# A decoder and PEER kernel on one core: the last attention's copies and splits in another order, the last four choices handed on one at a time, loops in TensorE's expert stage, and the final norm's weights spread on chip

## The chip, the core and the metric

The kernel runs on one core of a Trainium2 chip. The metric is device time in microseconds (us) of one execution, first to last instruction with what lies around them; the time before is the median of three runs. The core has five engines that run on their own and meet through semaphores: TensorE (PE in the profile; PEld is its weight load), VectorE (DVE), ScalarE (ACT), GpSimd (POOL) and SyncE (SP). Transfers run on 16 DMA engines.

## The reference, cut to what matters

The program is a two-layer block (pooling mixer, differential attention, four gated feed-forwards), followed by a second block: a hybrid attention mixer and a PEER layer that fetches expert rows by index. The change touches the mixer and the PEER layer of the second block and the last norm.

```python
def second_block(x, c, w_ada, b_ada, norm_attn, norm_ffn, w_in, w_out, rel_bias,
              peer_wq, peer_subkeys, peer_u, peer_v, norm_final):
    ...
        x = x + g1[:, None, :] * hybrid_mixer(h, w_in[l], w_out[l], rel_bias)
        h = modulate(rms_norm(x, norm_ffn[l]), sh2, sc2)
        x = x + g2[:, None, :] * peer_ffn(h, peer_wq[l], peer_subkeys[l], peer_u[l], peer_v[l])
    return rms_norm(x, norm_final)

def peer_ffn(h, w_query, sub_keys, u_emb, v_emb):
        ...
        e_idx = jnp.take_along_axis(cand_idx, pos, axis=-1)      # 128 experts for each of 256 tokens
        g = jax.nn.softmax(g_s, axis=-1)
        u = u_emb[e_idx]
        act = jax.nn.gelu(jnp.einsum('btd,bthkd->bthk', hc, u).astype(jnp.float32), approximate=False)
        return jnp.einsum('bthk,bthkd->btd', (g * act).astype(h.dtype), v_emb[e_idx])
```

All is float32, 256 tokens of width 1024. Every token picks 8 heads x 16 experts; each expert has a row of `u` and a row of `v`.

## The kernel before, in words

**Large products.** A weight chunk lands in `WR`; ACT writes its high part to `WH` (L1365) and DVE the rest to `WL` (L1877), half a chunk at a time. This is a *split*, in two pieces of 128x1024. PE then does three products per weight tile. `WH` and `WL` have two halves, so the split of half j + 2 waits until PE has used half j, and PE waits for the split. DVE copies a finished half out of PSUM (L1947, `post_copy`); PE may use that bank again, and the queries and keys in it, only then.

**The last attention** (L1160 to L1250 on PE, L1696 to L1746 on ACT, L2413 to L2474 on DVE) has 8 steps, each a pair of heads, pipelined by hand. In step i, PE does scores of pair i + 1 (L1167), the weighted sum of pair i - 1 (L1190, L1192) and the transposes of pair i (L1180, L1181). ACT does the exponentials (L1701), the normalising (L1710), the copy of the transposes (L1717, `pair_pt`) and of the result (L1721). DVE does bias and maxima (L2437, L2441) and the low part of the result (L2451), and beside these eight rounds of a selection of 64 keys, `topk` (L2419, L2422), three rounds per step. Between these each engine carries its share of halves 5 to 13 of the input product (steps 0 to 4), and in steps 5 to 7 of the output product. On each engine the order is that of the code: nothing is scheduled by a tool, every engine goes through its list and stops at each wait.

In step 0 DVE did three rounds of `topk`, then the copy of half 5 and the split of half 7, the copy of half 6 and the split of half 8. In steps 5 to 7 ACT did its part of a split ahead of `pair_pt`.

**The expert stage.** 64 groups (`GROUPS` is 32 for each of the two token tiles), each of 4 choices. POOL issues one indirect DMA per choice (L668): 128 rows of 8 KB, an expert's `u` beside its `v`. Four buffers of 4 choices each form a ring (`early_uv`, `late_uv`), and a gather waits until PE has used that buffer, four groups earlier (`v_used`). For a group DVE makes four dot products (L2525), each when its rows have landed; ACT takes one Gelu of the four (L1806); DVE multiplies by the gates (L2532); ACT writes four scaled identities `diag` (L1811); PE does eight products into PSUM (L1321, each in two passes, so 16 instructions). PE's code has groups 0 to 39 written out, then a loop of five rounds over groups 40 to 59, then groups 60 to 63 written out. DVE and ACT loop over groups 44 to 63.

**The end.** When tile 0's 32 groups are done, DVE adds them to `xt` and later scales by the final norm (`finish`); SP stores both halves of tile 0 as soon as they are ready. The norm's weights `gfin` come by one DMA that writes all 128 partitions (512 KB), issued when all choices are made. After group 63, `add_experts(1)` waits for all of PE's products, adds (L2577, L2578), ACT sums squares (L1844), DVE scales (L2585) and SP stores the second tile (L530).

## Time and profile before

| what | us |
|---|---|
| median of 3 runs (lowest to highest) | 1969.83 (1968.81 to 1976.73) |
| the profiled execution, device time | 1972.46 |
| its span, first to last instruction | 1971.2 |
| PE busy, share of the span | 1769.3, 90% |
| DVE busy, share of the span | 1280.4, 65% |
| ACT busy, share of the span | 799.0, 41% |

A share of busy time is a mean over stages with different limits. The chain that ended last is 57% PE and 25% DMA over the whole span; it is DMA in the last third, where the experts are fetched. What a step is worth is read from the stage it stands in: who waits there, for whom, and who waits for him.

### The profile page before, as it was taken

What the parts mean: (1) busy time and instruction counts of PE and PEld (TensorE: products, weight loads), DVE (VectorE), ACT (ScalarE), POOL (GpSimd) and SP (SyncE); (2) the same over time, 40 slices, a digit from 0 to 9 for tenths busy, and PEclk for the clock granted to TensorE, in tenths of its full rate; (3) what the DMA queues carried; (4) which work ended last, traced back from release to release, by engine and by line L of the source; (5) the groups of instructions that cost most, each with busy time, mean ns of one, the idle gap of its engine ahead of it and who ended that gap; (6) DMA issues with size and microseconds to landing.
All of it is one profiled execution on the core that took longest, in us unless ns stands there. A gap on an engine that the chain in (4) does not pass through costs nothing.

```text
span 1971.2 us, 23001 instructions
## 1 busy us (share of the span) xinstructions
PE 1769.3 (90%) x8104; PEld 1301.5 (66%) x8104; DVE 1280.4 (65%) x2235; ACT 799.0 (41%) x1442; POOL 651.3 (33%) x602
## 2 busy tenths in 40 slices
PE   7999999999999999999999889699888787878786
PEld 5887898888888888988887888575433333333232
DVE  4566866556465656676654676678688788855554
ACT  5444435544354436565443456442322232311111
POOL 4442551044214451144440012023443343333330
PEclk9999999999999999999999899899998888889999
DMA  8999985799999999769996965299999999999995
GB/s 261 319 363 392 316 289 219 262 337 366 334 321 334 373 348 343 265 224 312 353 355 220 280 209 163 87 385 351 394 419 420 419 420 420 419 421 421 420 421 215
DMA packets 247211, 650.00 MB, mean 330 GB/s; under 512 B 14881, under 2 KB 156498, under 8 KB 214354
## 3 DMA queue, kind: packets, MB, share of 16 engines
q1 hardware_dynamic: 200146, 346.15, 51.5%
q0 software_dynamic: 46304, 301.52, 38.3%
q10 hardware_dynamic: 672, 1.18, 0.3%
q8 instruction: 52, 0.85, 0.2%
q14 instruction: 37, 0.30, 0.0%
HBM read 643.56 MB, written 139.48 MB: 397 GB/s over the span
## 4 chain that ended last, share of the span: by engine, by line
PE 57%; DMA 25%; DVE 10%; ACT 4%; issue 3%; SPq 1%; POOL 0%; ACTq 0%; DVEq 0%
DMA late_uv<-uv_rows,M 11%; PE P L1321 9%; DMA early_uv<-uv_rows,M 7%; PE PX L828 6%; PE PX L830 6%; PE PX L829 6%; PE P L734 4%; PE P L736 4%; PE P L735 4%; DMA WR<-in_ffn_w_up 4%; DVE WL L1877 2%; PE P L683 2%; PE P L684 2%; PE P L685 2%; DMA WR<-in_ffn_w_down 2%
## 5 line engine op out<-in xcount | busy, mean ns | idle before, releaser
L1877 DVE TENSOR_TENSOR WL<-WR,WH 128x1024 fp32r<-128x1024 f32 (+1 forms) x246 | 325.2, 1363 | 205.4 <-ACT WH L1365 205.3
L1365 ACT ACTIVATE WH<-WR 128x1024 fp32r<-128x1024 f32 (+1 forms) x272 | 270.8, 1044 | 345.1 <-PE P L736 116.3
L1321 PE MATMUL P<-early_uv,M 128*128 128x512 f32 x576 | 284.7, 652 | 72.0 <-ACT M L1811 72.0
L828 PE MATMUL PX<-WH,hTh 128*128 128x512 f32 x704 | 280.7, 399 | 7.6 <-DVE WL L1885 5.1
L830 PE MATMUL PX<-WH,hTl 128*128 128x512 f32 x704 | 275.7, 392 | 0.0
L829 PE MATMUL PX<-WL,hTh 128*128 128x512 f32 x704 | 275.1, 391 | 0.0
L1321 PEld LDWEIGHTS P<-early_uv,M 128*128 128x128 f32 x576 | 117.3, 209 | 233.8 <-issue 143.1
L1321 PE MATMUL P<-late_uv,M 128*128 128x512 f32 x448 | 220.7, 651 | 55.3 <-ACT M L1811 55.0
L1892 DVE TENSOR_TENSOR WL<-WR,WH 128x1024 fp32r<-128x1024 f32 x128 | 177.8, 1430 | 138.4 <-ACT WH L1374 138.4
L668 POOL DMA_INDIRECT early_uv<-uv_rows,M x144 | 138.7, 963 | 297.1 <-PE P L1321 189.5
L2525 DVE CUSTOM_DVE_ANT_0 early_uv<-early_uv,PX 128x1024 f32<-128x1024 f32 x144 | 171.7, 1220 | 79.7 <-DMA early_uv<-uv_rows,M 79.0
L570 POOL TENSOR_TENSOR adaW<-adaW,silc 128x1024 f32<-128x1024 f32 x48 | 98.5, 2051 | 352.1 <-DMA adaW<-in_w_ada 352.1
L1321 PEld LDWEIGHTS P<-late_uv,M 128*128 128x128 f32 x448 | 90.5, 207 | 184.4 <-issue 108.3
L1806 ACT ACTIVATE lam<-lam 128x4 f32<-128x4 f32 x64 | 13.1, 205 | 462.9 <-DVE lam L2525 462.9
L1374 ACT ACTIVATE WH<-WR 128x1024 fp32r<-128x1024 f32 x128 | 128.6, 1052 | 175.9 <-PE PX L830 100.9
L734 PE MATMUL P<-WH,actH 128*128 128x512 f32 x472 | 188.9, 400 | 6.7 <-DVE WL L1877 5.0
L736 PE MATMUL P<-WH,actL 128*128 128x512 f32 x472 | 185.9, 394 | 0.0
L735 PE MATMUL P<-WL,actH 128*128 128x512 f32 x472 | 185.6, 393 | 0.0
L2525 DVE CUSTOM_DVE_ANT_0 late_uv<-late_uv,PX 128x1024 f32<-128x1024 f32 x112 | 134.1, 1220 | 67.4 <-DMA late_uv<-uv_rows,M 66.9
L668 POOL DMA_INDIRECT late_uv<-uv_rows,M x112 | 106.5, 951 | 166.2 <-PE P L1321 158.8
L828 PEld LDWEIGHTS PX<-WH,hTh 128*128 128x128 f32 x704 | 132.8, 189 | 37.9 <-issue 8.6
L830 PEld LDWEIGHTS PX<-WH,hTl 128*128 128x128 f32 x704 | 132.7, 189 | 28.7
(385 smaller groups left out, 3186.9 us busy)
## 6 DMA issues: line engine op xcount, KB each, us to landing
WR<-in_ffn_w_up SPq DMA_DIRECT2D x88, 1024.0 KB, 10.2
WR<-in_ffn_w_down SPq DMA_DIRECT2D x44, 1024.0 KB, 11.2
uv_rows<-in_peer_u SPq DMA_DIRECT2D x37, 1024.0 KB, 13.4
uv_rows<-in_peer_v SPq DMA_DIRECT2D x37, 1024.0 KB, 13.5
uv_rows<-in_peer_u SPq DMA_DIRECT2D x54, 512.0 KB, 9.9
uv_rows<-in_peer_v SPq DMA_DIRECT2D x54, 512.0 KB, 9.8
adaW<-in_w_ada POOLq DMA_DIRECT2D x48, 512.0 KB, 8.3
WR<-in_diff_w_in SPq DMA_DIRECT2D x14, 1024.0 KB, 11.5
```

The source lines that it names most:

```text
L668: pool.indirect_dma_start(rows_uv(n)[:, i, :], None, uv_rows, bass.IndirectOffsetOnAxis(ap=eidx[:, at:at + 1], axis=0)).then_inc(uv_landed ...
L734: mm(o, xh, WH[:, U % 2, w], start=first and kk == 0, stop=False)
L735: mm(o, xh, WL[:, U % 2, w], start=False, stop=False)
L736: return mm(o, xl, WH[:, U % 2, w], start=False, stop=last_half and kk == 1)
L828: mm(o, xh, WH[:, u, w], start=(k == 0), stop=False)
L829: mm(o, xh, WL[:, u, w], start=False, stop=False)
L830: return mm(o, xl, WH[:, u, w], start=False, stop=(k == KT - 1))
L1321: last = mm(P[2 * t + q][:], diag[:, n % 2, i], rows_uv(n)[:, i, D + q * 512:D + q * 512 + 512], start=n % GROUPS == 0 and i == 0, stop=n ...
L1365: nc.scalar.activation(split_view(WH, U % 2, kind, part), raw(c % 2, kind, h, part), copy)\
L1877: tt(split_view(WL, U % 2, kind, part), raw(c % 2, kind, h, part), split_view(WH, U % 2, kind, part).bitcast(F32), ALU.subtract)\
L1892: tt(split_view(WL, U % 2, "pair", part), raw(c % 2, "pair", h, part), split_view(WH, U % 2, "pair", part).bitcast(F32), ALU.subtract).the ...
L2525: last = nc.vector.tensor_tensor_reduce(out=u[:, i, 0:D], in0=u[:, i, 0:D], in1=HTOK[n // GROUPS], scale=1.0, scalar=0.0, op0=ALU.mult, op ...
```

## The change

Five things are changed.

1. DVE, step 0 of the last attention: after two rounds of `topk` come the copies of halves 5 and 6 and then the splits of halves 7 and 8; the third round stands behind them.
2. ACT, steps 5 to 7: `pair_pt` stands ahead of the split.
3. The last group of experts (63): for each of its four choices a Gelu, a gate product, one scaled identity and two products follow the dot product at once. PE counts the left halves of the output in `left_used` and the right ones in `v_used`, and the last addition waits for each half by itself. DVE and ACT get groups 60 to 62 written out for this.
4. PE: groups 12 to 31 and 33 to 60 are loops; 32 stands alone between them.
5. The final norm's weights land as one row of 4 KB, early, and PE spreads them over the partitions by a product with ones, ACT copies them to `gfin`; and SP holds the store of tile 0 back until PE has used groups 0 to 62.

```diff
-    gfin = view(MX + 6144, D)
+    gfin, gfrow = view(MX + 4096, D), view(MX + 5120, D)[0:1, :]
...
-        sp.wait_ge(S["index_ready"], len(ALL_CALLS))
-        sp.dma_start(gfin, a["norm_final_2"].partition_broadcast(128)).then_inc(S["gfin_landed"], 16)
+        sp.wait_ge(S["sk_scores"], 8)
+        sp.dma_start(gfrow, a["norm_final_2"].unsqueeze(0)).then_inc(S["gfin_landed"], 16)
         for t in range(2):
+            if t == 0:
+                sp.wait_ge(S["v_used"], 2 * GROUPS * NG - NG)
...
-        for n in range(EARLY, GROUPS + 8):
+        for n in range(EARLY, 12):
             experts(n)
-        with pe.Fori(0, GROUPS // 4 - 3) as r:
-            for n in range(GROUPS + 8, GROUPS + 12):
+        pe.wait_ge(S["gfin_landed"], 16)
+        for q in range(2):
+            last = mm(P[2 + q][:], ones[0:1, :], gfrow[:, q * 512:q * 512 + 512], start=True, stop=True)
+        last.then_inc(S["gfin_spread"], 1)
+        with pe.Fori(0, (GROUPS - 12) // 4) as r:
+            for n in range(12, 16):
                 experts(n, r)
-        for n in range(2 * GROUPS - 4, 2 * GROUPS):
+        pe.wait_ge(S["gfin_ready"], 1)
+        experts(GROUPS)
+        with pe.Fori(0, GROUPS // 4 - 1) as r:
+            for n in range(GROUPS + 1, GROUPS + 5):
+                experts(n, r)
+        for n in range(2 * GROUPS - 3, LAST):
             experts(n)
+        for i in range(NG):
+            pe.wait_ge(S["diag_ready"], LAST + i + 1)
+            for q in range(2):
+                mm(P[2 + q][:], diag[:, LAST % 2, i], rows_uv(LAST)[:, i, D + q * 512:D + q * 512 + 512], start=False, stop=i == NG - 1,
+                   skip_group_check=True).then_inc(S["v_used" if q else "left_used"], 1)
...
-            if i in OUT2_SLOTS:
-                split(phases["out2"]["U"] + OUT2_SLOTS[i] + 2)
...
             if i < PAIRS:
                 pair_pt(i)
+            if i in OUT2_SLOTS:
+                split(phases["out2"]["U"] + OUT2_SLOTS[i] + 2)
...
+            if n == 12:
+                act.wait_ge(S["gfin_spread"], 1)
+                for q in range(2):
+                    last = nc.scalar.activation(gfin[:, q * 512:q * 512 + 512], P[2 + q][:], copy)
+                last.then_inc(S["gfin_ready"], 1)
...
+        for i in range(NG):
+            act.wait_ge(S["dots_ready"], LAST + i + 1)
...
+            nc.scalar.activation(gel8[:, g, i:i + 1], dots[:, g, i:i + 1], ACT.Gelu).then_inc(S["gelu_ready"], 1)
+            act.wait_ge(S["coef_ready"], LAST + i + 1)
...
+            nc.scalar.activation(diag[:, g, i], ident[:], copy, scale=coef8[:, g, i:i + 1]).then_inc(S["diag_ready"], 1)
...
+                if i == 0 and n == 2:
+                    for j in (5, 6):
+                        post_copy(phases["in2"]["U"] + j, phases["in2"]["E"] + j, dest_in2(j), bank0("in2"))
+                    for j in (5, 6):
+                        split(phases["in2"]["U"] + j + 2)
+                    ahead, behind = [], []
                 if n < TOPK // 8:
                     topk(n)
...
-            dve.wait_ge(S["v_used"], NG * (t * GROUPS + GROUPS))
             if t:
                 dve.wait_ge(S["fss_ready"], 3)
+                dve.wait_ge(S["left_used"], NG)
+            else:
+                dve.wait_ge(S["v_used"], NG * GROUPS)
             for q in range(2):
                 c = slice(q * 512, q * 512 + 512)
+                if t and q:
+                    dve.wait_ge(S["v_used"], 2 * NG * GROUPS)
```

On DVE, in step 0 of the last attention, the third round of `topk` (MAX and two MATCH_REPLACE), the copies of two halves (COPY into the part of `M` that holds queries and keys) and the splits into `WL` stood in this order before:

```order
L2419 MAX small<-memK 128x8 x2
L2422 MATCH_REPLACE memK<-small,memK 128x128
L2422 MATCH_REPLACE memK<-small,memK 128x256
L1947 COPY M<-P 128x512
L1877 TENSOR_TENSOR WL<-WR,WH 128x1024 x2
L2447 RECIPROCAL st<-st 128x4
```

(The COPY and the TENSOR_TENSOR stand there twice, one pair for each half.) On the same engine at the same place they stand now, under the new line numbers:

```order
L1981 COPY M<-P 128x512 x2
L1911 TENSOR_TENSOR WL<-WR,WH 128x1024 x4
L2453 MAX small<-memK 128x8 x2
L2456 MATCH_REPLACE memK<-small,memK 128x128
L2456 MATCH_REPLACE memK<-small,memK 128x256
L2481 RECIPROCAL st<-st 128x4
```

The second copy has moved ahead of a split and of a round of `topk`; DVE's work in the step is the same.

On ACT, in step 5 of the last attention, behind the exponentials, the split into `WH` and the copy of the transposes (128x768, `pair_pt`) stood so before:

```order
L1701 ACTIVATE M,st<-M,st 128x128 x2
L1701 ACTIVATE M,st<-M,st 128x256 x2
L1365 ACTIVATE WH<-WR 128x1024 x2
L1717 ACTIVATE M<-PX 128x768
L1710 ACTIVATE M<-M,st 128x128 x2
```

And they stand so now:

```order
L1718 ACTIVATE M,st<-M,st 128x128 x2
L1718 ACTIVATE M,st<-M,st 128x256 x2
L1734 ACTIVATE M<-PX 128x768
L1382 ACTIVATE WH<-WR 128x1024 x2
L1727 ACTIVATE M<-M,st 128x128 x2
```

The copy and the split have changed places; in step 6 a load of the square root's table stands between the exponentials and both.

## Rows read from the trace of the kernel before

**Rows 1.** The page: the span, and GB/s in 40 equal slices.
```profile
span 1971.2 us, 23001 instructions
GB/s 261 319 363 392 316 289 219 262 337 366 334 321 334 373 348 343 265 224 312 353 355 220 280 209 163 87 385 351 394 419 420 419 420 420 419 421 421 420 421 215
```
**Rows 2.** Stretches: length, busy (x count) of PE PEld DVE ACT POOL, PEclk, DMA share, GB/s.
```profile
1550.00:1600.00 50.00, 39.43 (x78) 16.37 (x79) 40.51 (x112) 13.10 (x33) 17.52 (x19) 0.90 1.01 420
1948.00:1950.00 2.00, 2.00 (x4) 0.91 (x3) 1.23 (x2) 0.00 (x0) 0.00 (x0) 0.50 0.06 25
```
**Rows 3.** Timeline of DVE, dot products: start, duration, what [idle before <-releaser].
```profile
1547.93 1.22 DVE L2525 CUSTOM_DVE_ANT_0 late_uv<-late_uv,PX 128x1024 f32<-128x1024 f32 x1 [2.23 <-DMA late_uv<-uv_rows,M]
1557.90 1.22 DVE L2525 CUSTOM_DVE_ANT_0 early_uv<-early_uv,PX 128x1024 f32<-128x1024 f32 x1 [1.27 <-DMA early_uv<-uv_rows,M]
1953.28 1.22 DVE L2525 CUSTOM_DVE_ANT_0 late_uv<-late_uv,PX 128x1024 f32<-128x1024 f32 x1 [1.25 <-DMA late_uv<-uv_rows,M]
```
**Rows 4.** DMA queues, 1538 to 1552 us: packets, MB, share of 16 engines.
```profile
q14 instruction: 1, 0.01, 0.1%
```
**Rows 5.** DMA queues, 1550 to 1560 us, the same columns.
```profile
q8 instruction: 1, 0.02, 0.7%
```
**Rows 6.** DMA queues, 1773.7 to 1953.2 us: the only queue with packets.
```profile
q0 software_dynamic: 9955, 72.43, 97.2%
```
**Rows 7.** DMA queues and issues (count, KB, us to landing), 1420 to 1953 us.
```profile
q1 hardware_dynamic: 432, 1.05, 0.5%
q8 instruction: 4, 0.07, 0.0%
...
late_uv<-uv_rows,M POOLq DMA_INDIRECT x104, 27.6
...
M<-in_norm_final SPq DMA_DIRECT2D x1, 512.0 KB, 7.9
```
**Rows 8.** Timeline of PE, last attention, steps 0 and 1.
```profile
1155.76 0.38 PE L1180 MATMUL PX<-ident,M 128*128 128x128 f32 x2
1160.64 1.66 PE L1167 MATMUL PX<-M 64*128 64x128 f32 x8 [4.07 <-DVE M L1947]
1176.62 0.38 PE L1180 MATMUL PX<-ident,M 128*128 128x128 f32 x2
```
**Rows 9.** Timeline of DVE, last attention, steps 0 and 1.
```profile
1168.52 0.41 DVE L2422 MATCH_REPLACE8 memK<-small,memK 128x256 f32<-128x256 f32 x1
1170.14 0.69 DVE L1947 COPY M<-P 128x512 f32<-128x512 f32 x1 [1.21 <-PE P L724]
1173.44 0.42 DVE L2451 TENSOR_TENSOR actL<-PX,actH 128x256 fp32r<-128x256 f32 x1
1176.82 0.69 DVE L1947 COPY M<-P 128x512 f32<-128x512 f32 x1 [2.96 <-PE P L685]
```
**Rows 10.** Timeline of ACT, last attention, steps 5 and 6.
```profile
1224.23 2.00 ACT L1365 ACTIVATE WH<-WR 128x1024 fp32r<-128x1024 f32 x2 [1.82 <-PE P L736]
1226.14 0.79 ACT L1717 ACTIVATE M<-PX 128x768 f32<-128x768 f32 x1
...
1231.58 1.28 ACT L1736 ACT_TABLE_LOAD   x1
```
**Rows 11.** Timeline of PE, weighted sums of pairs 5 and 7.
```profile
1226.98 0.66 PE L1190 MATMUL PX<-M 128*64 128x256 f32 x4 [1.27 <-ACT M L1717]
...
1245.65 0.66 PE L1190 MATMUL PX<-M 128*64 128x256 f32 x4 [2.13 <-ACT M L1717]
```
**Rows 12.** Timeline of all engines, groups 62 and 63 and the end.
```profile
1946.54 8.83 PE L1321 MATMUL P<-late_uv,M 128*128 128x512 f32 x16 [2.77 <-ACT M L1811]
...
1955.17 1.28 ACT L1811 ACTIVATE M<-ident,lam 128x128 f32<-128x128 f32 x4 [0.42 <-DVE lam L2532]
...
1956.49 7.13 PE L1321 MATMUL P<-late_uv,M 128*128 128x512 f32 x16 [1.12 <-ACT M L1811]
...
1963.67 0.69 DVE L2577 TENSOR_TENSOR M<-P,g2bc 128x512 f32<-128x512 f32 x1 [8.61 <-PE P L1321]
```

More of the change, by code:

```diff
@@ L41 @@
 GROUPS = 128 // NG
+LAST = 2 * GROUPS - 1
 STOP = 99
@@ L215, in program @@
         sk_landed sk_tr sk_ready htok_tr htok_ready htok_moved sk_scores s_ready gdiff_ready gexp_ready gate_ready
-        index_ready dots_ready gelu_ready coef_ready diag_ready v_used g2_diag g2_tr g2_ready gfin_landed
+        index_ready dots_ready gelu_ready coef_ready diag_ready v_used left_used g2_diag g2_tr g2_ready gfin_landed gfin_spread gfin_ready
         update_done shifted_ready sqs_ready rstd_made xf_ready fss_ready fstd_ready y_ready stored peer_free""".split()
@@ L1855, in _ @@
                 gate_exps(CALL_AT[n])
+            if n == 12:
[3 more added lines that the diff above has]
+                last.then_inc(S["gfin_ready"], 1)
             if n == GROUPS + 3:
                 variance(0)
-        with act.Fori(0, GROUPS // 4 - 3) as r:
+        with act.Fori(0, GROUPS // 4 - 4) as r:
             for n in range(GROUPS + 12, GROUPS + 16):
                 experts(n, r)
+        for n in range(LAST - 3, LAST):
+            experts(n)
+        g = LAST % 2
+        for i in range(NG):
+            act.wait_ge(S["dots_ready"], LAST + i + 1)
+            if i == 0:
+                act.wait_ge(S["coef_ready"], LAST - 1)
+            nc.scalar.activation(gel8[:, g, i:i + 1], dots[:, g, i:i + 1], ACT.Gelu).then_inc(S["gelu_ready"], 1)
+            act.wait_ge(S["coef_ready"], LAST + i + 1)
+            if i == 0:
+                act.wait_ge(S["v_used"], NG * (LAST - 1))
+            nc.scalar.activation(diag[:, g, i], ident[:], copy, scale=coef8[:, g, i:i + 1]).then_inc(S["diag_ready"], 1)
         variance(1)
@@ L2457, in _ @@
                 pair_logits(i + 1)
+            ahead, behind = around(i)
             for n in range(3 * i, 3 * i + 3):
+                if i == 0 and n == 2:
[4 more added lines that the diff above has]
+                    ahead, behind = [], []
                 if n < TOPK // 8:
                     topk(n)
-            ahead, behind = around(i)
             for j in ahead:
@@ L2594, in _ @@
             if n == GROUPS + 11:
-                dve.wait_ge(S["gfin_landed"], 16)
+                dve.wait_ge(S["gfin_ready"], 1)
                 finish(0)
-        with dve.Fori(0, GROUPS // 4 - 3) as r:
+        with dve.Fori(0, GROUPS // 4 - 4) as r:
             for n in range(GROUPS + 12, GROUPS + 16):
                 experts(n, r)
+        for n in range(LAST - 3, LAST):
+            experts(n)
+        g, u = LAST % 2, rows_uv(LAST)
+        dve.wait_ge(S["gelu_ready"], LAST - 1)
+        for i in range(NG):
+            dve.wait_ge(uv_landed[ring(LAST)][i], 16 * turn(LAST))
+            nc.vector.tensor_tensor_reduce(out=u[:, i, 0:D], in0=u[:, i, 0:D], in1=HTOK[1], scale=1.0, scalar=0.0,
+                                           op0=ALU.mult, op1=ALU.add, accum_out=dots[:, g, i:i + 1]).then_inc(S["dots_ready"], 1)
+            dve.wait_ge(S["gelu_ready"], LAST + i + 1)
+            if i == 0:
+                dve.wait_ge(S["diag_ready"], LAST - 1)
+            at = LAST * NG + i
+            tt(coef8[:, g, i:i + 1], gel8[:, g, i:i + 1], gatec[:, at:at + 1], ALU.mult).then_inc(S["coef_ready"], 1)
         add_experts(1)
```

## The prediction

> **What bounds the kernel now.** I read the page first, then stretches, queues and single instructions where the change stands. The GB/s line [rows 1] splits the kernel: up to about 1280 us the rate goes up and down with the weights, then it is flat at 420 to the last slice. There the experts are fetched, with the DMA share at 1.01 while no engine is full: PE 39 of 50 us, DVE 41 [rows 2]. So the last third is set by bytes, and by when the fetching starts. The start is set by the last attention and what follows it, where PE and DVE wait for each other [rows 8, 9]. The end is set by what runs after the last rows have landed at 1953.28 [rows 3]; from there to the end of the span it is 17.9 us.
>
> One more reading: at 1948 to 1950 the DMA share is 0.06, one engine of 16, while DVE still waits for rows until 1953.28 [rows 2, 3]. One engine is late by some 5 us, and each gather is done only when it is. The lateness has a source that shows: around a code packet on q14 [rows 4] DVE sat idle 2.23 us before a dot product, where an undisturbed one has 1.27 [rows 3]: 0.96 us lost for every gather behind it. Around a code packet on q8 the idle time is 1.27, so nothing is lost [rows 5, 3]. q8 has four packets in the expert stage and none from 1773.7 on [rows 7, 6], while PE, DVE and ACT loop and POOL's code is still written out; I take q8 for PE's code.
> The Trainium skill (DMA: Bandwidth & Descriptors, "Why a DMA increments its semaphore by 16 and not by 1") says that only the full count means that all data have landed, since the engines finish independently. The trace agrees with its one late engine; by that rule code that is fetched through any other engine costs nothing.
>
> **The change, part by part.**
>
> *DVE's order in step 0 of the attention.* PE ended the transposes of pair 0 at about 1156.6 and then sat idle 4.07 us for DVE's copy of half 6 before the scores of pair 2 at 1160.64 [rows 8]. That copy stood behind a split and the third round of the selection. Now it follows the second round and the copy of half 5, both over by 1156.1, so the scores start near 1157 and PE has 3.7 us more. Not all of it is kept, since DVE is full from there to the end of the sixth round at 1168.9 [rows 9] and its work is the same. Half 7 is then done long before, so the copy goes at 1168.9 instead of 1170.14 (1.2 earlier), the split of half 9 ends at 1172.0 and the low part of result 0 at 1172.3 instead of 1173.85 [rows 9]. PE's transposes of pair 1 need that result: they go at 1172.4 instead of 1176.62 [rows 8], **4.2 us** earlier. The lower bound is 1.2: only DVE's first wait goes and PE finds another. The upper is what DVE waited for PE in step 1, 1.21 + 2.96 = 4.2 [rows 9]; I take that end, for PE has more than that to give. Behind step 1 the engines meet as before; the masks on POOL and the loads on SP move with the splits that release them.
>
> *ACT's order in steps 5 to 7.* The split held ACT 2.00 us from 1224.23, and `pair_pt` followed at 1226.14 [rows 10], though PE, through with its scores, had waited for it since 1225.7, 1.27 us [rows 11]; the wait two steps on is 2.13. With the copy first, pair 5 saves 1.2. In pair 6 the split and all behind it are 1.4 later, and the table load that ended at 1232.9 [rows 10] now ends at 1234.3 against transposes that end near 1233: the copy waits for it, and the running gain falls to 0.9. Pair 7 has nothing ahead of it: 1.2 again. Sum **2.1 us**; bounds 1.2 (the first wait alone) and 3.7 (three times). The splits moved back have a step to spare, and SP's loads behind them too.
>
> *Norm weights and store.* The norm's broadcast (512 KB) and tile 0's store (twice 256 KB) are the 1.05 MB of q1 in the expert stage [rows 7]. At 420 GB/s that is **2.5 us** of a stage in which all 16 engines are full. The broadcast becomes one row of 4 KB; the store moves behind group 62, when all rows have landed, and has some 10 us until tile 1's own store is due, so it is covered; without that cover it would cost its 1.25 us. The spread adds two products on PE, about four passes at the 0.45 of [rows 12] (7.13 / 16), two copies on ACT, and a wait of PE on the row with groups 12 on queued behind it. A gather takes 27.6 us from issue to landing and 2.5 of transfer [rows 7, 2]: the queue holds some 20 us of work, which hides 2 us of PE. Bounds 2.0 to 2.5.
>
> *The last group, one choice at a time.* Before, the four identities took 1.28 us from 1955.17 [rows 12] after the last dot product, then 16 passes 7.13 from 1956.49, and DVE went on at 1963.67 [rows 12]. Now the passes of the first three choices are ready before; but PE is still in group 62, which began at 1946.54 and took 8.83 at the lower clock level (0.50, 1.2 GHz [rows 2]), to 1955.4. So PE runs through from there: 1955.4 + 7.13 = 1962.5, a gain of 1.1; with group 62 at full clock it is 1953.7 + 7.13 = 1960.8, a gain of 2.8. The left half is handed on two passes (0.9) earlier, which saves about 0.85 in DVE's two pairs of operations. Together 2.0 to 3.7; I take **2.8**, since the row of group 63 has the full clock and 62 may have either. DVE's wait for each Gelu holds only the next dot product, due 2.5 us later; the round trip is 1.22 + some 0.6.
>
> *PE's loops* save two or three packets of q8, and those cost nothing [rows 3, 5]: **0**. Loop branches cost nothing either where PE waits for ACT anyway. Bounds: a gain of up to 5 us if this code goes through the late engine, a loss as under the third rival.
>
> **Sum:** 4.2 + 2.1 + 2.5 + 2.8 = 11.6 us; by the bounds 1.2 + 1.2 + 2.0 + 2.0 = 6.4 to 4.2 + 3.7 + 2.5 + 3.7 = 14.1. The profiled execution took 1972.46 for a span of 1971.2, so it would take 1960.9; it lies 2.6 above the median of the runs, 1969.83, from which I forecast **1958.2**, by the bounds 1955.7 to 1963.4.
>
> **The rivals.** *DVE stays the bound of the attention.* It is full in step 0 and half of step 1 [rows 9], and 4.2 us is the whole of what it waited; if PE's earlier halves only change where it waits, or PE falls to the lower clock in a new gap, 1.2 is left of that term: a saving of 8.6, 1961.2. For it speaks that DVE's list there is no shorter; against it that PE's 4.07 us were the longest wait.
>
> *PE's code goes through the late engine.* Then two to three packets fewer, 16 KB each at 0.96 per 8 KB, give 1.9 each, up to the 5 us by which that engine is late: 1953. Against it stands the undisturbed 1.27 [rows 3, 5].
>
> *The loops fetch their code again in each round: slower.* Twelve rounds at 1.9 us are 23 us on one engine. Up to 5 of it are free if it is not the late one: 18 us more, 1976, and PE would wait for its code besides. It outweighs all gains from nine rounds on. Against it: five rounds of the old loop without a q8 packet [rows 6]; for it: the new loops lie elsewhere in the code.
> The Trainium skill (Advanced Engine Details and Errata, "ISA Cache") gives TensorE 128 KB in lines of 256 instructions. By that a loop of four groups, with some 140 instructions, stays resident and this rival falls; the trace agrees with its 16 KB packets and the quiet loop. For the other engines the skill has a line of the same size; the packet on q14 is half that (0.01 MB), and the measurement decides.
>
> *The copies can't go earlier*, since half 6 is not done: it ended before 1156, so this has no chance of its own.
>
> **How the numbers follow.** The forecast has a chance of 0.66, the first rival 0.21, the second 0.06, the third 0.04; 0.03 is for what I don't see. About 0.5%, 9.85 us, is what a measurement of this kernel can tell from no change, so faster means below 1960.0. Of the forecast's own range about eight tenths lie below that (0.53), with all of the second rival (0.06) and a fifth of the first (0.04): faster 0.63. Slower is the third rival: 0.04. Same is the rest, 0.33. Runs of before lie between 1968.81 and 1976.73, so the range takes in a run to run shift of 3 us at either end: 1952 to 1967. The third rival is left out.
>
> **What would show it.** DVE's order: PE's wait before the scores of pair 2 under 0.6 us, and the first gather about 6 us earlier than before. ACT: no wait of PE for pair 5, still one of 1.5 to 2.5 for pair 6, under 1.1 for pair 7. Bytes: no q1 packets of that size between 1420 us and the last landing. Tail: PE without a gap from group 62 to the end of 63, and 14 to 16 us from the last landing to the end. The loops: fewer q8 packets and the same 2.49 us between dot products. What would make it wrong: a first gather less than 3 us earlier, q8 packets in the loops, or an engine later than before at the last landing.

## The result, and the profile after

The changed kernel took 1961.33 us, the kernel before 1969.35 beside it (medians of 10 runs each): ratio 0.9947, interval 0.9933 to 0.9961. A second comparison, later, gave 0.9947 (0.9928 to 0.9965). So it is faster by 7.7 to 13.2 us, where 11.6 was forecast, and its median lies 3.1 above the forecast of 1958.2. It is also above 1960.0, the line below which the prediction would call it faster, though the interval excludes 1. The profiled execution took 1964.30 for a span of 1962.9, 8.3 less than before. Its head, against [rows 1]:

```profile
span 1962.9 us, 23045 instructions
...
GB/s 262 323 362 386 339 280 218 262 339 359 337 318 338 372 339 337 293 213 298 356 349 224 282 203 196 70 375 354 388 419 421 419 420 420 420 420 420 421 420 259
```

The flat rate is the same. So I cut both traces at events that both have: the transposes of pair 0 in the last attention, the landings of the gathers, and the end. Gather n is the n-th of the 256 indirect transfers, four to a group. It is spread over 16 DMA engines and has landed when the last of them is done. All rows up to gather 256 go by the first engine that is done; the lag is the time from the first engine to the last.

| from ... to | forecast | before | after | difference |
|---|---|---|---|---|
| start to transposes of pair 0 | 0 | 1155.76 | 1157.01 | +1.25 |
| to gather 1, first engine | -6.3 | 125.13 | 121.03 | -4.10 |
| gather 1 to gather 33, first engine | 0 | 105.35 | 106.66 | +1.31 |
| gather 33 to gather 168, first engine | 0 | 336.92 | 336.81 | -0.11 |
| gather 168 to gather 192, first engine | -2.5 | 62.32 | 59.85 | -2.47 |
| gather 192 to gather 256, first engine | 0 | 159.60 | 159.59 | -0.01 |
| gather 256, first engine to last (the lag) | 0 | 8.19 | 8.07 | -0.12 |
| last landing to the end (the tail) | -2.8 | 17.97 | 13.91 | -4.06 |

Nothing of the change lies ahead of pair 0: over all 14 traces of this study that point lies between 1148.8 and 1159.4. This scatter of 10 us is the reason why a time alone tells little here; the distances behind it tell far more. They scatter too: from pair 0 to gather 1 the four traces that have the attention of before (before, b3, b4, b5 of the table below) take 125.1 to 127.8 us, the five with that of the changed kernel 119.4 to 121.0. The trace of before in this table is the shortest of its four, so the -4.10 is at the low end: the means of the two sets, 126.1 and 120.6, are 5.5 apart. Between gathers 33 and 256 the distances of kernels with the same code there repeat within 0.4 us.

PE in steps 0 and 1, which answers to [rows 8] (start, duration, what, idle before it and releaser):

```profile
1157.01 0.38 PE L1183 MATMUL PX<-ident,M 128*128 128x128 f32 x2
...
1158.17 0.93 PE L1170 MATMUL PX<-M 64*128 64x128 f32 x8 [0.35 <-DVE M L1981]
...
1165.17 0.66 PE L1193 MATMUL PX<-M 128*64 128x256 f32 x4
...
1173.68 0.41 PE L1183 MATMUL PX<-ident,M 128*128 128x128 f32 x2 [1.70 <-DVE actL L2485]
...
1174.46 1.24 PE L1170 MATMUL PX<-M 64*128 64x128 f32 x8
```

The wait of 4.07 us is 0.35, and pair 1 stands 16.67 us behind pair 0 instead of 20.86. But PE now waits 1.70 for the low part of result 0, and the scores behind that wait take 1.24, where those at 1158.17 took 0.93. The weighted sums of pairs 5, 6 and 7 (before, they waited 1.27, 2.13 and 2.13 us; 5 and 7 are in [rows 11]):

```profile
1224.34 0.66 PE L1193 MATMUL PX<-M 128*64 128x256 f32 x4
...
1233.77 0.66 PE L1193 MATMUL PX<-M 128*64 128x256 f32 x4 [2.23 <-ACT M L1734]
...
1241.88 0.66 PE L1193 MATMUL PX<-M 128*64 128x256 f32 x4 [0.90 <-ACT M L1734]
```

The DMA queues from 1420 to 1949 us (packets, MB, share of 16 engines) have lost q1 and its 1.05 MB, against [rows 7]:

```profile
q0 software_dynamic: 30077, 218.99, 99.8%
q14 instruction: 11, 0.09, 0.0%
q8 instruction: 2, 0.03, 0.0%
```

And the end, PE in groups 62 and 63 and DVE's last dot product and first addition, against [rows 12]:

```profile
1942.11 7.13 PE L1324 MATMUL P<-late_uv,M 128*128 128x512 f32 x16 [1.15 <-ACT M L1828]
1949.08 7.03 PE L1364 MATMUL P<-late_uv,M 128*128 128x512 f32 x16
```
```profile
1949.05 1.22 DVE L2650 CUSTOM_DVE_ANT_0 late_uv<-late_uv,PX 128x1024 f32<-128x1024 f32 x1 [0.83 <-DMA late_uv<-uv_rows,M]
...
1955.36 0.69 DVE L2621 TENSOR_TENSOR M<-P,g2bc 128x512 f32<-128x512 f32 x1 [4.65 <-PE P L1364]
```

PE runs from 1942.11 to 1956.11 without a gap. When the last rows land (1949.03) it has only begun with group 63: the tail is now PE's backlog.

### The profile page after: what moved, and what is told of

It is laid out like the page before. It is cut to its first block, busy times and chain, and to the rows that moved or that the text cites. A ratio compares the mean times of both kernels' runs of the same rounds, so it can differ in the third digit from the quotient of the medians.

```text
span 1962.9 us, 23045 instructions
## 1 busy us (share of the span) xinstructions
PE 1769.9 (90%) x8108; PEld 1302.1 (66%) x8108; DVE 1280.7 (65%) x2238; ACT 801.0 (41%) x1447; POOL 652.1 (33%) x602
## 4 chain that ended last, share of the span: by engine, by line
PE 54%; DMA 25%; DVE 10%; ACT 4%; issue 3%; POOL 3%; SPq 0%; ACTq 0%; DVEq 0%; POOLq 0%
DMA early_uv<-uv_rows,M 12%; PE P L1324 9%; PE PX L831 5%; PE PX L833 5%; PE PX L832 5%; DMA late_uv<-uv_rows,M 5%; PE P L737 4%; PE P L739 4%; PE P L738 4%; DMA adaW<-in_w_ada 4%; DMA WR<-in_ffn_w_up 3%; PE P L686 2%; PE P L687 2%; PE P L688 2%; DVE WL L1911 2%
## 5 line engine op out<-in xcount | busy, mean ns | idle before, releaser
L1324 PE MATMUL P<-late_uv,M 128*128 128x512 f32 x432 | 212.2, 649 | 52.0 <-ACT M L1828 51.9
L2565 DVE CUSTOM_DVE_ANT_0 late_uv<-late_uv,PX 128x1024 f32<-128x1024 f32 x108 | 129.0, 1219 | 60.8 <-DMA late_uv<-uv_rows,M 60.2
## 6 DMA issues: line engine op xcount, KB each, us to landing
uv_rows<-in_peer_u SPq DMA_DIRECT2D x37, 1024.0 KB, 13.9
```

The source lines that it names most:

```text
L1324: last = mm(P[2 * t + q][:], diag[:, n % 2, i], rows_uv(n)[:, i, D + q * 512:D + q * 512 + 512], start=n % GROUPS == 0 and i == 0, stop=n ...
L2565: last = nc.vector.tensor_tensor_reduce(out=u[:, i, 0:D], in0=u[:, i, 0:D], in1=HTOK[n // GROUPS], scale=1.0, scalar=0.0, op0=ALU.mult, op ...
```

## The experiments

Six questions: which part brings what (five kernels, each the kernel before with one part), whether DVE's list still holds the attention back, which code goes through the late engine, what the held store is worth, whether the backlog at the end can go, and whether the gains add. Intervals of the times are 0.3 to 0.6% wide, so the distances in the traces decide, one trace for each kernel. In the table, "pair 0 to 1" goes from the transposes of pair 0 to those of pair 1; the other columns are as in the table above.

| kernel | median us | ratio, interval | pair 0 to 1 | pair 0 to gather 1 | gather 168 to 192 | last landing to end |
|---|---|---|---|---|---|---|
| before | 1969.35 | 1 | 20.86 | 125.13 | 62.32 | 17.97 |
| after | 1961.33 | 0.9947, 0.9933 to 0.9961 | 16.67 | 121.03 | 59.85 | 13.91 |
| b1_dve_order | 1968.71 | 0.9985, 0.9967 to 1.0004 | 16.69 | 121.28 | 62.33 | 17.97 |
| b2_act_order | 1968.07 | 0.9994, 0.9977 to 1.0010 | 20.55 | 123.31 | 62.33 | 17.96 |
| b3_norm_row | 1968.34 | 0.9988, 0.9968 to 1.0009 | 19.78 | 125.86 | 59.85 | 19.65 |
| b4_last_group | 1963.96 | 0.9974, 0.9954 to 0.9995 | 21.08 | 125.62 | 62.36 | 15.58 |
| b5_pe_loops | 1971.54 | 0.9998, 0.9981 to 1.0015 | 20.49 | 127.81 | 62.33 | 17.97 |
| after_again | 1961.89 | 0.9947, 0.9928 to 0.9965 | 16.68 | 121.00 | 59.85 | 15.63 |
| f_store_at_once | 1959.81 | 0.9948, 0.9923 to 0.9972 | 16.68 | 119.44 | 61.07 | 15.61 |
| c_rounds_233 | 1953.93 | 0.9913, 0.9896 to 0.9930 | 15.20 | 118.09 | 59.84 | 13.93 |
| d_dve_written_out | 1955.69 | 0.9917, 0.9901 to 0.9934 | 16.67 | 120.84 | 59.85 | 15.57 |
| e_three_groups | 1956.36 | 0.9916, 0.9892 to 0.9939 | 16.68 | 120.85 | 59.85 | 10.99 |
| best | 1954.18 | 0.9919, 0.9889 to 0.9949 | 15.19 | 119.93 | 59.84 | 10.99 |
| best_2 | 1953.20 | 0.9912, 0.9881 to 0.9943 | 15.19 | 118.07 | 59.85 | 10.99 |

b1 to b4 ran on one chip, b5, c, d and e on another, after_again, f, best and best_2 on the first again; on which chip the first two rows ran is not on record. The changed kernel itself was not timed on the second chip. There d, which is the changed kernel with something added that costs 1 us, has 0.9917, against 0.9947 for the changed kernel elsewhere. So the ratios of c and e (0.9913 and 0.9916) don't show that they are faster than the changed kernel: by time c, d and e are the same, and what c and e gain rests on their traces.

Of the times that were expected, those of c and d were 6 and 8 us too high; the others came within 4.

### DVE's order alone

```diff
+            ahead, behind = around(i)
             for n in range(3 * i, 3 * i + 3):
+                if i == 0 and n == 2:
+                    for j in (5, 6):
+                        post_copy(phases["in2"]["U"] + j, ...)
+                    for j in (5, 6):
+                        split(phases["in2"]["U"] + j + 2)
+                    ahead, behind = [], []
...
-            ahead, behind = around(i)
```

> The kernel before with the new order of DVE in step 0 alone. Both theories: PE's wait of 4.07 us before the scores of pair 2 falls under 0.6, and from the transposes of pair 0 to those of pair 1 it is 16.7 us instead of 20.9 (4.2 less). Theory A (the gain is kept): from the transposes of pair 0 to the first row of the first gather it is 4.2 us less than before (121 instead of 125.1), and the time is 1965.1. Theory B (part of it goes back to the clock): in step 1 PE now waits some 1.7 us for the low part of result 0, falls to the lower clock level, and its next half of the input product takes 7.2 us instead of 6.0; 1.9 to 2.7 us are left at the first gather, and the time is 1966.7 to 1967.4.

By the trace theory A holds and theory B does not: 16.69 us from pair 0 to pair 1, 64.10 to pair 5 (before 68.27), and at the first gather 121.28, 3.85 less than before; the time (0.9985, interval up to 1.0004) can't tell it from no change. The four other traces with the old order of DVE have 19.8 to 21.1 us to pair 1 and 67.2 to 68.5 to pair 5, so against them the gain at pair 1 is 3.1 to 4.4; at the first gather the 3.85 is the least, since the other three with the old attention stand at 125.6 to 127.8. PE waited 1.71 us for the low part as in the changed kernel, but behind that wait its clock stayed. The same eight microseconds in both (length, busy of PE, PEld, DVE, ACT, POOL, granted clock, DMA share, GB/s), after and then b1:

```profile
1172.70:1180.70 8.00, 7.02 (x46) 6.24 (x47) 7.86 (x20) 5.49 (x15) 0.00 (x0) 0.79 0.85 259
```
```profile
1172.50:1180.50 8.00, 7.01 (x58) 6.54 (x59) 7.86 (x20) 5.50 (x15) 0.00 (x0) 1.00 0.84 258
```

With 46 matmuls in place of 58 in the same time, the changed kernel lost 1.5 us here: pair 5 stood at 65.62 instead of 64.10. Five traces have this wait besides (b1, after_again, d, e, f); in all five pair 5 stands at 64.1. And part of the 4.2 was itself clock. In the kernel before, the scores of pair 2 and the first 4 us of the half of the input product behind them ran at the lower of the two levels (0.50, 1.2 GHz), behind the 4.07 us in which PE had stood idle; after, they run at 1.00. All five traces with the old order of DVE (before, b2, b3, b4, b5) have the lower level there, for 3.4 to 6.8 us, and none of the nine with the new order.

```profile
1160.00:1166.00 6.00, 5.36 (x25) 4.74 (x26) 5.93 (x13) 2.72 (x10) 2.01 (x4) 0.50 0.86 255
```
```profile
1159.20:1165.20 6.00, 5.98 (x50) 5.85 (x50) 5.90 (x12) 2.23 (x6) 0.00 (x0) 1.00 0.65 194
```

The weighted sum of pair 0, which stands behind that half, was at 1169.96 before and is at 1165.17 after:

```profile
1169.96 0.66 PE L1190 MATMUL PX<-M 128*64 128x256 f32 x4
```

From the transposes of pair 0 that is 14.20 and 8.16 us, so PE is 6.0 earlier there: 3.7 of it is the wait that went (4.07 to 0.35), 2.3 the clock. From there to the transposes of pair 1, with the new wait of 1.70 for DVE's low part, it takes 1.85 longer than before, and 4.2 are left.

### ACT's order alone

```diff
-            if i in OUT2_SLOTS:
-                split(phases["out2"]["U"] + OUT2_SLOTS[i] + 2)
...
             if i < PAIRS:
                 pair_pt(i)
+            if i in OUT2_SLOTS:
+                split(phases["out2"]["U"] + OUT2_SLOTS[i] + 2)
```

> The kernel before with ACT's copy of the transposes ahead of its split in steps 5 to 7, alone. Theory: PE's wait before the weighted sum goes from 1.27 to about 0 for pair 5, stays 2.1 to 2.3 for pair 6 (the load of the square root's table), and goes from 2.13 to 0.9 for pair 7: 2.4 us less from the transposes of pair 5 to the end of the last half of the output product. Rival A: the splits that now stand behind the copy come too late for PE, which waits for WH or WL in its place: under 1 us is left. Rival B (clock): what follows the attention is set by DVE and by the clock, so 1.6 or less of it is left at the first gather. Time 1967.0 by the theory, 1968.4 by rival A, 1967.8 by rival B.

The waits came as the theory said: none for pair 5, 2.24 for pair 6, 0.90 for pair 7. From the start of the transposes of pair 5 to the end of the output product it is 2.37 us less (26.23 instead of 28.60). Rival A falls, since PE waits for no split. Rival B came true: 1.56 is left at the start of the next large product, because the first tile's product of 24 matmuls, 4.65 us before, takes 5.46 here. Before and then b2 (granted clock third from the end):

```profile
1258.30:1263.00 4.70, 4.65 (x24) 4.48 (x24) 4.20 (x13) 2.27 (x8) 0.00 (x0) 0.62 0.00 0
```
```profile
1255.50:1261.00 5.50, 5.46 (x24) 5.17 (x24) 4.17 (x13) 1.98 (x7) 0.00 (x0) 0.50 0.00 0
```

It stands 2.9 us behind the start of the eight transposes ahead of it in both, since it waits for DVE, and here it is at the lower clock as a whole; before, part of that stretch fell on the eight transposes (1.97 us instead of 1.09), and PE still waited 0.94 behind them. All nine traces with this order of ACT have 5.3 to 5.5 there, the five others 4.6 to 4.9.

### The norm's weights and the held store

```diff
-        sp.dma_start(gfin, a["norm_final_2"].partition_broadcast(128)).then_inc(S["gfin_landed"], 16)
+        sp.wait_ge(S["sk_scores"], 8)
+        sp.dma_start(gfrow, a["norm_final_2"].unsqueeze(0)).then_inc(S["gfin_landed"], 16)
         for t in range(2):
+            if t == 0:
+                sp.wait_ge(S["v_used"], 2 * GROUPS * NG - NG)
```

(with PE's spread and ACT's copies at group 12 as in the change.)

> The kernel before with the norm's weights as one row that PE spreads, and with tile 0's store held until groups 0 to 62 are used. Theory: in the expert stage only bytes count, so from gather 168 to gather 192 the landing is 2.5 us earlier than before against the gathers ahead, and nowhere else does anything change; the time is 1966.9. Rival A: the wait of PE for the row and the spread (two products, two copies) at group 12 holds the ring, and the landings of the gathers behind are later by 1 to 2 us before they are earlier by 2.5: 1968 to 1969. Rival B: the held store ends after tile 1's own and makes the end later by its 1.2 us: 1968.1.

The theory holds: 59.85 us from gather 168 to 192 instead of 62.32, and 336.82 from 33 to 168, where the spread lies, so its cost is hidden (rival A falls). The tail is 1.7 longer, but not through the store (rival B): PE took 8.77 us for group 63 instead of 7.13 [rows 12], with 3.4 us of it at the lower clock level.

```profile
1954.02 8.77 PE L1323 MATMUL P<-late_uv,M 128*128 128x512 f32 x16 [2.82 <-ACT M L1820]
```

f is the changed kernel without SP's wait ahead of the store of tile 0:

```diff
-            if t == 0:
-                sp.wait_ge(S["v_used"], 2 * GROUPS * NG - NG)
```

> The changed kernel without SP's wait before the store of tile 0, which is then written as soon as it is ready, among the gathers. Theory (only bytes count there): gathers from 180 on land 1.2 us later than in the changed kernel (61.1 us from gather 168 to 192 instead of 59.85), the tail is the same, 1.2 us more. Rival: the held store costs as much in the tail, where it meets the end: the tail is 1 us shorter and the time the same.

With the store back among the gathers, 1700 to 1770 us has it on q1, where the changed kernel has no such row:

```profile
q1 hardware_dynamic: 288, 0.52, 1.9%
...
out<-xt SPq DMA_DIRECT2D x2, 256.0 KB, 9.3
```

It costs 1.22 us of landing (61.07 against 59.85), and the tail is the same, 15.61 against 15.63 of after_again. So the 2.47 are half the store's and half the broadcast's, and the place it was moved to is free. The time doesn't show the 1.2: the median is 2.1 lower (1959.81 against 1961.89), but its interval (0.9923 to 0.9972) takes in that of after_again (0.9928 to 0.9965).

### The last group alone

```diff
+        for i in range(NG):
+            pe.wait_ge(S["diag_ready"], LAST + i + 1)
+            for q in range(2):
+                mm(P[2 + q][:], diag[:, LAST % 2, i], ...).then_inc(S["v_used" if q else "left_used"], 1)
```

(and ACT, DVE and the last addition as in the change.)

> The kernel before with the last group's four choices handed on one by one, and the two halves of the output counted apart. Theory: from the last landing to the end of the span it is 13.9 to 14.1 us instead of 17.9 where PE has the full clock in groups 62 and 63 (PE runs through from 62 to the end of 63), 15.6 where group 62 is at the lower level; time 1965.3 to 1967. Rival: the code written out for groups 60 to 62 costs DVE one more code packet ahead of the last landing, which is then 1 us later (last engine 9.2 us behind the first instead of 8.2): 1966.3 to 1968.

Group 62 fell to the lower level, and the tail has 15.58, the forecast's 15.6; the late engine is 7.84 behind the first, so the rival falls.

```profile
1938.19 8.83 PE L1322 MATMUL P<-late_uv,M 128*128 128x512 f32 x16 [2.85 <-ACT M L1817]
1946.86 7.03 PE L1353 MATMUL P<-late_uv,M 128*128 128x512 f32 x16
```

Of the six traces with this tail (after, after_again, b4, c, d, f) two have group 62 at full clock and 13.9, four have the lower level and 15.6.

### TensorE's loops alone

```diff
-        for n in range(EARLY, GROUPS + 8):
+        for n in range(EARLY, 12):
             experts(n)
-        with pe.Fori(0, GROUPS // 4 - 3) as r:
-            for n in range(GROUPS + 8, GROUPS + 12):
+        with pe.Fori(0, (GROUPS - 12) // 4) as r:
+            for n in range(12, 16):
                 experts(n, r)
-        for n in range(2 * GROUPS - 4, 2 * GROUPS):
+        experts(GROUPS)
+        with pe.Fori(0, GROUPS // 4 - 1) as r:
+            for n in range(GROUPS + 1, GROUPS + 5):
+                experts(n, r)
+        for n in range(2 * GROUPS - 3, 2 * GROUPS):
             experts(n)
```

> The kernel before with TensorE's groups 12 to 31 and 33 to 60 as loops, alone. Theory: nothing. PE has fewer code packets on q8 in the expert stage (2 or 3 instead of 5 between 1410 and 1953 us), the dot products stay 2.49 us apart, the last engine of the last gather stays 7.7 to 8.2 us behind the first, and the time is that of before, 1970. Rival A: PE's code goes through the late engine, which then lands 1.9 to 4 us less behind the first, and the time is 1966 to 1968. Rival B: the loops fetch their code again, more q8 packets than before, 1976.

Nothing, as the theory said: 1971.54 against 1970.83. From 1420 to 1953 us there is one packet on q8, where [rows 7] has four, at 1641.2, and the dot products around it are 2.50 us apart, the second after the undisturbed wait of 1.27:

```profile
q8 instruction: 1, 0.02, 0.0%
```
```profile
1640.21 1.22 DVE L2529 CUSTOM_DVE_ANT_0 early_uv<-early_uv,PX 128x1024 f32<-128x1024 f32 x1 [1.27 <-DMA early_uv<-uv_rows,M]
1642.71 1.22 DVE L2529 CUSTOM_DVE_ANT_0 early_uv<-early_uv,PX 128x1024 f32<-128x1024 f32 x1 [1.27 <-DMA early_uv<-uv_rows,M]
```

The late engine is 7.70 behind the first; the kernels with PE's code written out have 7.72 (b1) to 8.19 (before). Both rivals fall: three packets fewer take nothing from the late engine, and the loops do not fetch again. In the changed kernel one q8 packet (1552.9) falls into the rounds of the first loop: one, and not one for each round.

### DVE's loop written out

```diff
-        with dve.Fori(0, GROUPS // 4 - 4) as r:
-            for n in range(GROUPS + 12, GROUPS + 16):
-                experts(n, r)
-        for n in range(LAST - 3, LAST):
+        for n in range(GROUPS + 12, LAST):
             experts(n)
```

> The changed kernel with VectorE's loop over groups 44 to 59 written out: some 310 more instructions of code, nothing else. Theory (VectorE's code packets on q14 go through the engine that lands last): two or three more q14 packets between 1760 and 1949 us, the last engine of the last gather 10.0 to 11.0 us behind the first instead of 8.1, the first engine's landing where it was; 2 to 3 us more, 1963.5. Rival (that engine is late for another reason, its lag only happens to grow in steps): the lag stays at 8.1 and the time at 1961.

The queues from 1870 to 1885 us, and the dot products there:

```profile
q0 software_dynamic: 866, 6.29, 101.3%
q14 instruction: 1, 0.01, 0.1%
```
```profile
1875.61 1.22 DVE L2565 CUSTOM_DVE_ANT_0 early_uv<-early_uv,PX 128x1024 f32<-128x1024 f32 x1 [1.15 <-DMA early_uv<-uv_rows,M]
1879.07 1.22 DVE L2565 CUSTOM_DVE_ANT_0 early_uv<-early_uv,PX 128x1024 f32<-128x1024 f32 x1 [2.23 <-DMA early_uv<-uv_rows,M]
1881.57 1.22 DVE L2565 CUSTOM_DVE_ANT_0 early_uv<-early_uv,PX 128x1024 f32<-128x1024 f32 x1 [1.26 <-DMA early_uv<-uv_rows,M]
```

My count was wrong: one packet came, not two or three (it lies 12 groups behind the one before, at 1756.3; my 310 instructions came from stretches in which DVE also sorts). The price was right: at that packet (1877.0) the dot product waits 2.23 us, and the last engine's lag behind the first steps from 7.91 to 8.88 and stays there to the last gather. Only DVE's code differs, so this packet is DVE's, and it costs 0.97 us of the end. The rival falls. The time does not show it: 2 to 3 us more were expected, 1955.69 was measured, and the changed kernel was not timed on this chip.

Not every packet on q14 costs that much. From 1490 us on the kernel before has nine; behind six of them (1495.9, 1544.6, 1601.7, 1643.8, 1693.4, 1757.7) the lag has a step of 0.96 to 0.98, or 1.2 at the last, beside the store; behind the three others (1562.8, 1702.2, 1705.3) it has none. Whose code those three are is not shown. At the last gather of before the other 15 engines are done within 2.70 us, the late one at 8.19, so 5.5 us of the end are its lag alone; no run took a packet of DVE away.

### One round of the selection later

```diff
-            for n in range(3 * i, 3 * i + 3):
-                if i == 0 and n == 2:
-                    ...
-                if n < TOPK // 8:
-                    topk(n)
+            for n in range(max(3 * i - 1, 0), min(3 * i + 2, TOPK // 8)):
+                topk(n)
+            if i == 0:
+                ... copies of halves 5 and 6, splits of 7 and 8
```

> The changed kernel with one round of the selection moved once more: two rounds in step 0, three in steps 1 and 2 (before: three, three, two), so that the low part of result 0 is done 1.4 us earlier. Theory A (DVE's list in steps 0 and 1 is what PE waits for): PE's wait before the transposes of pair 1 falls from 1.5 to 1.7 us to about 0.2, these stand 15.2 to 15.4 us behind those of pair 0 instead of 16.7, and the 1.4 us are kept up to the first gather (119.6 us from the transposes of pair 0 instead of 121.0); time 1960. Theory B (DVE stays the bound): the third round that is now in step 2 delays the next copy there, PE waits for that, and 0 to 0.3 us are left at the transposes of pair 5 (65.3 to 65.6 us from pair 0); time 1961.

```profile
1166.92 0.41 PE L1183 MATMUL PX<-ident,M 128*128 128x128 f32 x2 [0.23 <-DVE actL L2485]
```

PE's wait falls from 1.7 to 0.23, pair 1 stands at 15.20. At pair 5 it is 62.98 against 64.10: of 1.5 us 1.1 are kept, 0.19 are a new wait in step 2. So between the theories, nearer to A: DVE's list in steps 0 and 1 was still what PE waited for. The 118.09 at the first gather are better than this explains; best, with the same attention, has 119.93, with 3.4 us at the lower clock level behind the transposes of pair 6 that c does not have.

### Three groups one choice at a time

```diff
-        for n in range(2 * GROUPS - 3, LAST):
+        for n in range(2 * GROUPS - 3, 61):
             experts(n)
-        for i in range(NG):
-            ...
+        for n in range(61, LAST + 1):
+            for i in range(NG):
+                pe.wait_ge(S["diag_ready"], 61 + (n - 61) * NG + i + 1)
+                ...
```

(and the same on ACT and DVE.)

> The changed kernel with groups 61 and 62 handed on one choice at a time too. Theory A (the tail of the changed kernel is PE's backlog: PE is in group 62 until the last landing and has 16 passes left): PE works groups 61 to 63 off as they land, waits between choices, and ends about 3 us after the last landing instead of 7.1; from the last landing to the end of the span it is 10 to 10.5 us instead of 13.9; time 1957.5. Theory B: PE, waiting between choices, falls to the lower clock and needs 0.9 us for two passes instead of 0.45 each, and the round trips of Gelu hold the dot products: 12 us or more.

PE's last passes, the last dot product and the first addition:

```profile
1939.19 1.98 PE L1365 MATMUL P<-late_uv,M 128*128 128x512 f32 x4 [0.39 <-ACT M L1900]
...
1941.68 1.98 PE L1365 MATMUL P<-late_uv,M 128*128 128x512 f32 x4 [0.51 <-ACT M L1900]
...
1942.51 1.22 DVE L2657 CUSTOM_DVE_ANT_0 late_uv<-late_uv,PX 128x1024 f32<-128x1024 f32 x1 [1.32 <-DMA late_uv<-uv_rows,M]
...
1944.65 1.98 PE L1365 MATMUL P<-late_uv,M 128*128 128x512 f32 x4 [0.99 <-ACT M L1900]
1945.88 0.69 DVE L2627 TENSOR_TENSOR M<-P,g2bc 128x512 f32<-128x512 f32 x1 [1.72 <-PE P L1365]
```

PE now waits for the choices of group 63, and works the last off 4.1 us after its rows landed. From the last landing to the end it is 10.99, in three traces to the hundredth (e, best, best_2): theory A, though it forecast 3 us for PE and 10 to 10.5 for the tail. In all three the clock is at its upper level from before the last landing to PE's end.

### Both together, and ACT's order in steps 3 and 4 too

> The changed kernel as it is, beside the next three on one chip. Before had 1970 us in all comparisons; by the first comparison this has 0.9947 of it, 1959.6. From the transposes of pair 0 to the first gather 120.8 to 121.3 us; in step 1 PE stands 1.5 to 1.7 us before the transposes of pair 1, and whether the clock falls behind that gap is open (it fell in one of three traces with it: 65.6 instead of 64.1 us from pair 0 to pair 5).

best is c and e in one kernel.

> The changed kernel with both versions that gained: rounds of the selection two, three, three, and groups 61 to 63 handed on one choice at a time. If the gains lie apart (attention and tail), they add: 118 to 119.6 us from the transposes of pair 0 to the first gather, 10.2 to 11 us from the last landing to the end, 5 us less than the changed kernel, 1954.5. If not (the earlier tail falls into another clock level or the store of tile 0 collides with it), 2 to 3 us less.

best_2 adds this on ACT:

```diff
+            if 3 <= i < PAIRS:
+                pair_pt(i)
             for j in behind:
                 split(phases["in2"]["U"] + j + 2)
-            if i < PAIRS:
+            if i < 3:
                 pair_pt(i)
```

> As the last one, and ACT's copy of the transposes ahead of its split in steps 3 and 4 too. Theory (the same as in steps 5 to 7): PE's waits of 1.2 and 1.3 us before the weighted sums of pairs 3 and 4 go, the transposes of pair 5 stand 2.4 us nearer to those of pair 0 (60.6 us instead of 63.0), and about 2 of it reach the first gather; 1952.5. Rival: the split that is 0.8 us later there delays DVE's split, its reciprocal for the next pair and ACT's normalising, and PE waits 1.2 us at the transposes in place of the sums: nothing gained, 1954.5.

The weighted sums of pairs 3 and 4, in c (the order of the changed kernel) and in best_2:

```profile
1198.70 0.66 PE L1193 MATMUL PX<-M 128*64 128x256 f32 x4 [1.18 <-ACT M L1734]
...
1208.32 0.66 PE L1193 MATMUL PX<-M 128*64 128x256 f32 x4 [1.27 <-ACT M L1734]
```
```profile
1194.63 0.66 PE L1193 MATMUL PX<-M 128*64 128x256 f32 x4
1203.00 0.66 PE L1193 MATMUL PX<-M 128*64 128x256 f32 x4
```

Both waits are gone; pair 5 stands at 60.96 instead of 62.98, so 2.0 of 2.4 are kept there (DVE's low part and pair 5's copy now hold PE 0.21 and 0.42). Whether they reach the first gather is open: best_2 has 118.07 there, best 119.93, but c, with the attention of best, has 118.09. By time: after_again 1961.89 (1955.08 to 1967.99), best 1954.18 (1951.20 to 1958.22), best_2 1953.20 (1946.98 to 1960.82), before 1971.08. Both medians are below the changed kernel's, by 7.7 and 8.7 us, with runs and intervals that still overlap. From pair 0 to the end it is 807.28, 802.16 and 796.97 in the three traces. Of the 5.2 between best and best_2, 3.1 lie between gathers 1 and 33, where the two have the same code. And c and e, with one of the two parts each, have 800.3 and 799.7 there, less than best with both. So the parts add where each was made (15.19 us to pair 1, 10.99 in the tail); that they add in the time is not shown, nor that best_2 is faster than best.

## Why the prediction was right, and where not

The time fell within the range, and each part moved the place that the prediction named. But the median, 1961.33, lies on the time of the first rival (1961.2), not on the forecast (1958.2), by another way than that rival's: of DVE's term not 1.2 was left at pair 1 but 4.2, and what the trace lacks against the forecast went to the clock and to scatter, as told below.

*What bounds the kernel* held: bytes in the last third, the last attention ahead of it, the tail behind it. Of the stretches of the first table in which the change moves nothing, three stayed within 0.12 us; the two others are the scatter ahead of pair 0 and the clock between gathers 1 and 33.

*DVE's order*: 4.2 at pair 1, forecast and measured. DVE's side of the working came out: it put the end of the low part of result 0 at 16.5 us behind the transposes of pair 0, and it is 16.5 there (1173.12 + 0.41):

```profile
1173.12 0.41 DVE L2485 TENSOR_TENSOR actL<-PX,actH 128x256 fp32r<-128x256 f32 x1
```

The sentence that had no ground is that PE has more than 4.2 to give: its own number was 3.7. PE had 6.0, because its clock no longer fell behind the wait, and the forecast had no term for that. So the size is in part luck: had the clock fallen as before, PE and not DVE would have set pair 1, and by the prediction's own numbers some 3.7 (an estimate) would have been left. The new wait of PE, 1.70, was not given a number. The first rival named a new gap and the lower clock in it, and priced it too high: it came in one trace of six, and cost 1.5 there.

*ACT's order*: 2.1 forecast, 2.37 in b2, pairs 5 and 7 as said; pair 6 lost 0.1 and not 0.3.

*What reaches the first gather* is the weakest step: I carried 6.3 through, and against the one trace of before 4.1 came (4.1, 4.1, 4.3, 4.3 and 5.7 in the five traces with this attention). Against the mean of the four traces with the old attention it is 5.1 to 6.7. What can be named is clock: 0.8 goes where the first tile's product now falls to the lower level (b2), and 1.5 goes to one stretch at the lower level, behind the 1.70 us (after) or behind the 2.23 us of pair 6 (after_again, d and e); f has neither. That second loss is not the new order's alone: b3 and b5, with the old one, have 3.4 us at the lower level at the same place. Pair 6's sums and what follows in after_again and in f:

```profile
1234.50:1242.50 8.00, 7.91 (x32) 6.07 (x33) 2.87 (x4) 3.69 (x8) 0.00 (x0) 0.79 0.60 174
```
```profile
1227.00:1235.00 8.00, 7.20 (x38) 5.65 (x38) 2.87 (x4) 4.37 (x9) 0.00 (x0) 1.00 0.62 188
```

Counted from the start of the span the first gather came 2.84 us earlier (1278.04 against 1280.88), under the 3 that the prediction gave as a sign of being wrong; 1.25 of that is lost ahead of pair 0, where nothing changed.

*Norm weights and store*: 2.5 forecast, 2.47 in b3 and in the changed kernel, 1.22 of it the store's; the spread is hidden.

*The last group*: 2.8 forecast, 4.06 measured. The mechanism was right, the size was off because I put one value over two cases: with group 62 at the lower clock the tail is 2.4 shorter, at full clock 4.1. For the full clock my own terms were 2.8 + 0.85 for the left half; I took 2.8.

*PE's loops* and the late engine: 0, as forecast (b5), and the reading that DVE's packets, not PE's, delay the end was confirmed by adding one (d). The second and third rivals are excluded.

*The sum*: 11.6 forecast, 8.3 in the trace: 2.2 too much in the attention, 1.3 too little at the end, 1.31 lost to the clock between gathers 1 and 33, and 1.25 to the scatter ahead of pair 0. The last group's surplus hides a part of the attention's shortfall.

## What to carry to other kernels

When an engine's longest wait is removed, look up what that engine reads next and who makes it: here the copy went forward and the low part, one round of the selection later on the same list, was the next wait, and moving one more round gave 1.1 us more at pair 5. A hand-over in pieces pays only as far back as the receiver has a backlog: with one group PE ended 7.1 us after the last landing, with three groups 4.1. And where a transfer counts only when all its engines are done, find the late one and what else it carries, before shortening any other engine's code.

## What the runs showed of the hardware

The granted clock moves the time by about as much as a part of this change, and not in every execution at the same place. Between gathers 1 and 33 nothing differs in code, and the 14 traces take 103.0 to 106.8 us; before, after and e took 105.35, 106.66 and 103.34. The same 17 us in each, some 75 us behind gather 1 (PE's busy time first, granted clock third from the end):

```profile
1355.00:1372.00 17.00, 13.66 (x30) 5.75 (x29) 16.35 (x43) 3.91 (x9) 6.87 (x7) 0.90 0.95 350
```
```profile
1353.00:1370.00 17.00, 13.12 (x26) 5.52 (x24) 16.38 (x42) 3.91 (x9) 6.23 (x7) 0.80 0.85 323
```
```profile
1349.00:1366.00 17.00, 13.86 (x47) 7.23 (x46) 16.39 (x42) 3.91 (x9) 8.51 (x8) 1.00 0.92 355
```

All 14 traces sort that way: 103.0 to 104.1 us where this stretch has no lower clock, 105.3 to 106.1 at a mean of about 0.9, 106.1 to 106.8 at 0.8. DVE is busy for over 16 of the 17 us in the three shown, PE for 13 to 14. What decides in which execution the level falls stays open; no run here settles it.
